# Block transposes on VectorE and another row order of the weights in a mixture-of-experts layer

## The reference, cut to what matters

```python
def clamped_swiglu(gu):
    gate, up = gu[..., :D_FF], gu[..., D_FF:]
    gate = jnp.minimum(gate, 7.0)
    up = jnp.clip(up, -7.0, 7.0)
    return (up + 1.0) * (gate * jax.nn.sigmoid(gate * 1.702))

# 32 experts, each token goes to its 4 best; D_MODEL = D_FF = 1024
def expert_block(args):
    xblk, e = args
    act = clamped_swiglu(xblk @ w_gate_up[e] + b_gate_up[e])   # 1024 -> 2048 -> 1024
    return act @ w_down[e] + b_down[e]
```

## Time and profile before

| | us |
|---|---|
| three runs, median (lowest to highest) | 1427.42 (1425.87 to 1429.18) |
| the profiled execution, its device time | 1427.33 |
| its span, first to last instruction | 1425.6 |
| experts, first to last matmul of L661 and L687 | 321.96 to 1386.4 |
| PE busy | 1286.2 (90%) |
| DVE / ACT / POOL busy | 496.2 / 324.7 / 299.4 |
| moved by DMA | 454.86 MB, mean 319 GB/s |

### The profile page before, as it was taken

One profiled execution on the slowest core, in us unless ns is written; L12 is line 12 of the kernel. 1 busy time (PEld: TensorE's weight loads), 2 busy tenths in 40 slices (PEclk: granted clock), 3 DMA queues, 4 the chain that ended last, 5 costly groups with the idle time before them and its releaser, 6 DMA issues.

```text
span 1425.6 us, 33985 instructions
## 1 busy us (share of the span) xinstructions
PE 1286.2 (90%) x12484; PEld 560.1 (39%) x12485; DVE 496.2 (35%) x1476; ACT 324.7 (23%) x649; POOL 299.4 (21%) x348
## 2 busy tenths in 40 slices
PE   6999999959998999999999999888999899988870
PEld 3764544543333434444444333333443333433320
DVE  2002222443334333333333344342334333343337
ACT  2023332221312222222222222221223222222211
POOL 0513332011212212222212112130212212111210
PEclk9999999969999999999999999999999999999995
DMA  9512110224999999999989999998999989999967
GB/s 379 208 59 74 60 74 1 104 83 173 415 386 415 394 413 395 368 365 366 366 366 365 392 418 416 417 416 352 366 367 417 413 362 414 393 417 416 417 248 294
DMA packets 90869, 454.86 MB, mean 319 GB/s; under 512 B 14049, under 2 KB 14489, under 8 KB 55774
## 3 DMA queue, kind: packets, MB, share of 16 engines
q1 hardware_dynamic: 77902, 430.86, 74.5%
q0 software_dynamic: 12512, 22.11, 4.3%
q10 hardware_dynamic: 432, 1.57, 0.3%
HBM read 444.23 MB, written 14.71 MB: 322 GB/s over the span
## 4 chain that ended last, share of the span: by engine, by line
PE 73%; DMA 21%; DVE 3%; issue 1%; ACT 1%; POOL 0%; SPq 0%; DVEq 0%; POOLq 0%
PE bank L661 35%; DMA arena<-in_w_gate_up 20%; PE bank L687 14%; PE bank L421 7%; PE bank L491 4%; PE bank L437 3%; PE bank L648 2%; PE bank L626 2%; PE bank L706 1%; PE bank L450 1%; DVE xs L1284 1%; PE bank L478 1%; PE bank L464 1%; PE bank L707 1%; PE bank L616 1%
## 5 line engine op out<-in xcount | busy, mean ns | idle before, releaser
L661 PE MATMUL bank<-arena,hT 128*32 128x512 f32 x5120 | 583.9, 606 | 30.2 <-DMA arena<-in_w_gate_up 27.9
L687 PE MATMUL bank<-arena,hT 128*32 128x256 f32 x5120 | 308.4, 386 | 33.1 <-ACT hT L859 33.1
L661 PEld LDWEIGHTS bank<-arena,hT 128*32 128x32 f32 x5120 | 157.3, 111 | 393.0 <-issue 341.1
L1241 DVE TENSOR_TENSOR arena<-bank,gain 128x512 f32<-128x512 f32 x128 | 88.4, 691 | 402.0 <-PE bank L661 402.0
L687 PEld LDWEIGHTS bank<-arena,hT 128*32 128x32 f32 x5120 | 159.6, 111 | 161.3 <-issue 77.3
L963 POOL DMA_DIRECT2D ahead<-in_consts x98 | 51.6, 530 | 641.1 <-DVE hT L1260 615.3
L876 ACT ACTIVATE arena<-arena 128x256 f32<-128x256 f32 x128 | 53.3, 417 | 560.1 <-DVE arena L1243 558.7
L1260 DVE TENSOR_TENSOR hT<-bank,gain 128x256 f32<-128x256 f32 x128 | 51.4, 422 | 212.2 <-PE bank L687 206.1
L980 POOL DMA_INDIRECT y_rows<-hT,arena x80 | 82.4, 1029 | 158.3 <-DVE hT L1260 150.7
L421 PE MATMUL bank<-hT,arena 128*128 128x512 f32 x224 | 103.6, 610 | 0.8 <-ACT hT L764 0.8
L966 POOL DMA_INDIRECT hT<-h_rows,arena x82 | 84.8, 1035 | 67.9 <-issue 34.0
(11 more groups left out here) (146 smaller groups left out, 857.9 us busy)
## 6 DMA issues: line engine op xcount, KB each, us to landing
arena<-in_w_gate_up SPq DMA_DIRECT2D x256, 1024.0 KB, 6.6
arena<-in_w_down SPq DMA_DIRECT2D x128, 1024.0 KB, 15.3
arena<-in_w_in SPq DMA_DIRECT2D x10, 1024.0 KB, 18.1
arena<-y_rows SPq DMA_DIRECT2D x8, 1024.0 KB, 12.3
arena<-in_w_out SPq DMA_DIRECT2D x4, 1024.0 KB, 22.0
arena<-bias_by_dist POOLq DMA_DIRECT2D x6, 512.0 KB, 4.0
xs<-in_x SPq DMA_DIRECT2D x4, 512.0 KB, 7.4
h_rows<-arena POOLq DMA_DIRECT2D x4, 512.0 KB, 2.9
```

The source lines that it names most:

```text
L661: mm = pe.matmul(bank[c][j * CH:(j + 1) * CH, :].rearrange("p (g n) -> p g n", g=2), xT[:, c, (k % 2) * P + (k // 2) * CH:(k % 2) * P + (k ...
L687: mm = pe.matmul(bank[c][j * CH:(j + 1) * CH, 0:Q], aT[:, c, (k % 2) * P + (k // 2) * CH:(k % 2) * P + (k // 2 + 1) * CH], w[:, j * Q:(j + ...
L1241: dve.tensor_tensor(gu[:, b, :], bank[c][:, :], bt[:, 0:2 * Q], ALU.add).then_inc(gu_read, 1)
```

## The change

PE no longer transposes or multiplies biases in the jobs, and ACT no longer copies. DVE turns each chunk with one instruction that transposes 32 x 32 blocks, SBUF to SBUF. A block transpose leaves quarter j on partitions 32 j to 32 j + 31. With its input read at a step of eight values (32 bytes), what stands on partition p for step k is weight row 8 p + k, so the weights are read in that order: partition p of gate unit k holds weight row 8 p + k (8 KB, from one partition to the next 64 KB apart in HBM), and of down unit u rows 8 p + 2 u and 8 p + 2 u + 1 (8 KB in one piece, 32 KB apart). The biases of one expert are fetched by a DMA of four rows of 3 KB, issued by ACT, and spread over the 32 partitions of each quarter by one DVE shuffle of 128 x 768. Chunks that are absent do no work on any engine: the semaphores count chunks, not four for each job, and two more rows of the job table carry the running counts. Each engine loads more of them into registers in a job: PE three instead of one, DVE six instead of two. The rows of the next job are turned on DVE between the last activation and `job_columns`.

```diff
@@ load_unit @@
-                    src = w_gate_up[bass.ds(e, 1), u * P:(u + 1) * P, :].rearrange("e p n -> p (e n)")
-                    dst = ring[:, u, :]
+                    src = w_gate_up[bass.ds(e, 1)].rearrange("e (p k) n -> (e k) p n", p=P)[u]
                 else:
-                    a = (u - KT) * 2 * P
-                    src = w_down[bass.ds(e, 1), a:a + 2 * P, :].rearrange("e (k p) n -> p (e k) n", p=P)
-                    dst = ring[:, u, :].rearrange("p (k n) -> p k n", k=2)
+                    src = w_down[bass.ds(e, 1)].rearrange("e (p u k) n -> (e u) p (k n)", p=P, k=2)[u - KT]
+                dst = ring[:, u, :]
@@ PE, run_job @@
-                pe.wait_ge(t_copied, job * NCH + 1)
-                pe.wait_ge(pick_done, job + 1)
-                pe.matmul(bank[4][:, 0:2 * Q], pick, bias_all[:, 0:2 * Q], start=True, stop=True).then_inc(bias_mm, 1)
-                pe.matmul(bank[5][:, 0:Q], pick, bias_all[:, 2 * Q:3 * Q], start=True, stop=True).then_inc(bias_mm, 1)
-                pe.wait_ge(x_copied, job * 2 + 2)
+                every = range(KT)
                 indices(job + 1)
+                pe.wait_ge(x_done, job + 1)
                 with pe.If(chunks > 2):
                     with pe.If(chunks > 3):
                         gate(3, every)
...
+                    gate(2, every)
+                gate(1, every)
+                gate(0, every)
                 with pe.If(chunks > 2):
                     with pe.If(chunks > 3):
                         down(3, every)
...
+                    down(2, every)
+                down(1, every)
                 down(0, every)
             njobs = pe.value_load(njobs_i[0:1, 0:1], min_val=E, max_val=JOBS_MAX - 2)
             with pe.Fori(0, njobs) as job:
-                run_job(job, pe.value_load(jobs_i[0:1, 2, bass.ds(job, 1)], min_val=1, max_val=NCH))
+                run_job(job, pe.value_load(jobs_i[0:1, 2, bass.ds(job, 1)], min_val=LEAST, max_val=NCH),
+                        pe.value_load(jobs_i[0:1, 3, bass.ds(job, 1)], min_val=2, max_val=COUNT_MAX),
+                        pe.value_load(jobs_i[0:1, 3, bass.ds(job + 1, 1)], min_val=4, max_val=COUNT_MAX))
@@ ACT @@
+            def load_bias(e):
+
+                act.dma_start(bias_row[0:P:CH, :], biases[bass.ds(e * 4, 4), :])\
+                    .then_inc(bias_in, 16)
...
+                act.wait_ge(bias_spread, job + 1)
+                load_bias(e)
@@ DVE @@
+            def flip_x(c, last):
+
+                ins = dve.transpose(xT[:, c, :], xg[:, c, :].rearrange("p (i k) -> p k i", k=KT))
...
+                def swiglu(c):
...
+                    dve.tensor_tensor(act_q[b], up, sg[:, b, :], ALU.mult).then_inc(actq_done, 1)
+                    dve.wait_ge(actq_done, low + (AHEAD - c))
+                    dve.transpose(aT[:, c, :], act_q[b].rearrange("p (i k) -> p k i", k=KT)).then_inc(act_done, 1)
...
+                dve.wait_ge(y_done, before_job + AHEAD)
+                dve.wait_ge(bias_in, job * 16 + 16)
+                dve.stream_shuffle(bt, bias_row[:, :], [0] * CH).then_inc(bias_spread, 1)
+                job_rows(job + 1, link_job)
+                dve.wait_ge(bias_spread, job + 1)
+                with dve.If(chunks > 2):
+                    with dve.If(chunks > 3):
+                        swiglu(3)
+                    swiglu(2)
+                swiglu(1)
+                swiglu(0)
+                dve.wait_ge(gathered, rows_in)
+                with dve.If(next_chunks > 2):
+                    with dve.If(next_chunks > 3):
+                        flip_x(3, False)
+                    flip_x(2, False)
+                flip_x(1, False)
+                flip_x(0, True)
                 job_columns(after, job + 2, link_job)
-                for c in range(NCH):
-                    dve.wait_ge(scattered[c], job * 16 + 16)
+                dve.wait_ge(scattered, before_job * 16)
...
-                for n, c in enumerate(ORDER):
-                    dve.wait_ge(dn_done, job * NCH + (n + 1))
+                with dve.If(chunks > 2):
+                    with dve.If(chunks > 3):
+                        add_bias(3)
+                    add_bias(2)
+                add_bias(1)
+                add_bias(0)
```

More of the change, by code:

```diff
@@ L65 @@
 FREED = JOB_UNITS - 2
-ORDER = tuple(range(NCH))[::-1]
+LEAST = 2
+AHEAD = NCH - 1
 JOBS_MAX = 49
+COUNT_MAX = 2 + NCH * JOBS_MAX
 FAR = 4096
@@ L672, in gate, with down @@
                             mm.then_inc(units_used, 1)
-                        if k == 5 and flip is not None:
-                            flip_act(flip)
-                def down(c, ks, absent=0):
-                    n = ORDER.index(c)
-                    if 0 in ks:
-                        pe.wait_ge(t_copied, job * NCH + (n + 2))
+                def down(c, ks):
+                    pe.wait_ge(act_done, low + (AHEAD - c))
                     for k in ks:
@@ L903, in link @@
                 pool.wait_ge(pstep, steps[0])
-            for c in range(NCH):
-                pool.dma_start(ahead[0:16, 1, c, :], consts[0:16, 4 * c:4 * c + 4])\
-                    .then_inc(scattered[c], 16)
+            for a in range(2):
+                pool.dma_start(ahead[0:16, a, :], consts[0:16, 4 * a:4 * a + 4]).then_inc(scattered, 16)
+            pool.memset(bias_row[:, :], 0.0).then_inc(bias_zero, 1)
             link(pool.memset(pb[:, :, 0:8], 0.0))
@@ L998, in _ @@
                 pool.sem_inc(waited_pool, 1)
-                gather(next_chunks)
-                for n, c in enumerate(ORDER):
-                    pool.wait_ge(y_done, job * NCH + (NCH + n + 2))
-                    pool.sem_inc(waited_pool, 1)
-                    if c == 0:
-                        scatter_chunk(c)
-                        continue
-                    with pool.If(chunks > c):
-                        scatter_chunk(c)
-                    with pool.If(chunks <= c):
-                        signal(c, scattered[c], 1)
@@ L1010, in _ @@
-            for c in range(NCH):
-                pool.wait_ge(gathered[c], njobs * 16 + 16)
+                with pool.If(next_chunks > 2):
+                    with pool.If(next_chunks > 3):
+                        gather(3, gathered)
+                    gather(2, gathered)
+                gather(1, gathered)
+                gather(0, gathered)
+                with pool.If(chunks > 2):
+                    with pool.If(chunks > 3):
+                        scatter(3)
+                    scatter(2)
@@ L1217, in _ @@
                 .then_inc(gate_in, 1)
+            def flip_x(c, last):
+                ins = dve.transpose(xT[:, c, :], xg[:, c, :].rearrange("p (i k) -> p k i", k=KT))
+                if last:
+                    ins.then_inc(x_done, 1)
+            dve.wait_ge(gathered_first, 16 * NCH)
+            for c in range(NCH):
+                flip_x(c, c == NCH - 1)
             job_columns(1, None, link)
-            job_picker(0)
             link(dve.tensor_copy(keep_s, idx_t[:, :, 1]))
```

261 lines of the change are left out of this document (103 added, 158 removed).

## The result

The changed kernel takes 1406.28 us (median of 4 runs, 1404.44 to 1407.78) where the kernel before, run beside it, takes 1426.91 us: ratio 0.9853, 95% interval 0.9835 to 0.9871. It is 20.6 us faster, less than half of the 45 us that the prediction gave it: about 25 us of the forecast gain are missing. The profiled execution took 1407.16 us with a span of 1405.4 us.

The account below looks back on a forecast made before the run. PE was taken to bound three-chunk jobs, weight transfers two-chunk jobs. Stage -39 us, last job -4.3 and start -1.5, together -45 against 1427.33, gave 1382 us; range 1357 to 1412.

Parts of the forecast that it names:

- The likeliest case: Whole kernel: the forecast itself holds, with a time of 1370 to 1400 us; chance 0.60.
- the case that did hold 1400 to 1424: Whole kernel: DVE or gathers as a partial bound, or a pitch that costs up to 3%; chance 0.13.
- the pitch: Rival, weight transfers: 64 KB steps could collide in HBM, 1481 us at 10%; slower by this or long DVE chain, chance 0.10.
- the idle at a job's start: PE at each job start: two more register loads leave the array idle about 0.65 us, 1.0 at most.
- just in time: Three-chunk job after a handover: SP issues at 9.3 us, DMA has down units for 10.5 us, data follows within 2 us.
- The stage: First free gate slot to last handover: 968 us for bytes plus 4 and 14 us, 986 us, or -39.
- The array's own work: PE in a three-chunk job without flips and bias matmuls: 31.4 to 31.9 us, taken as 31.5.
- The lead of 0.3 us: PE's sequencer at a job start: runs some 0.3 us ahead, set against 0.97 us for two more loads.
- DVE as the bound: Rival: PE waits for DVE once a transpose takes 1.55 us; 1424 us at 2.2 us, half of it 1403.
- No effect: Rival, whole kernel: saved PE time is lost to waits one for one, 1427 us; chance 0.03.
- The floor of DMA alone: Rival, whole kernel: loads hidden, clock up, down units gain, only bytes count, 1357 us; chance 0.14.
- its 4 and 14: Stage: 8 three-chunk jobs behind three-chunk jobs at 32.1 instead of 31.6, 4 us; 7 behind two-chunk jobs at 2 us, 14.

Follow-up runs that it names:

- the first experiment: Changed kernel with only the chunk count loaded at a job's start, two table loads moved between gate groups and the bias-add wait moved too: 1393.67 us.
- The filler: Changed kernel with 20 unused matmuls placed between and behind the three register loads at each job start on PE: 1406.68 us, ratio 0.9841.
- the experiment on the row order: Kernel before with only the new order of weight rows in its transfers, output not the reference's: 1418.11 us, ratio 0.9944.
- slots and late loads: Changed kernel with second slots for gate units 0 to 5, gate code in two arms, and two table loads moved off the job start: 1364.56 us.
- the two failed forms of spare slots: Changed kernel with six more ring slots and SP and PE loops unrolled by two: 1485.19 us; the same with table loads moved off the job start: 1536.41 us.

## Why the prediction was wrong, point by point

The direction held, and so did part of the mechanism: PE lost its flips and biases and three-chunk jobs became shorter, by 2.1 us. 1406 us is inside the range of 1357 to 1412, but by luck. The likeliest case, 1370 to 1400, missed, and the case that did hold 1400 to 1424 rested on DVE or the pitch, which had no part in it. Two steps failed. The first is the idle at a job's start: 0.6 us were taken and the array stands for 1.7 us, with a slow clock behind it in some jobs, where the prediction had the clock fall behind waits for weights alone. Gaps at a job's start far from 0.6 us were one of its own signs of being wrong. The second is the rest of DMA that comes from one slot for each unit: it was taken at 2 us, and "just in time" otherwise, and is 3.8 us in a pair of jobs. The profiled execution is 25.2 us over 1382. The terms, one by one:

**The stage.** Forecast 986 us from the first free slot to the last handover; the trace has it from 337.87 to 1351.17, 1013.3 us, 27 us more. It falls into two parts and a rest.

*Three-chunk jobs behind three-chunk jobs*, forecast 32.1 us, measured 33.84: 8 x 1.74 = 14 us. Three errors lie in it.
- The array's own work: from a gate start to the end of down 31.17 us and 0.55 for the index matmuls, so 31.7, where 31.5 was taken: 0.2 us.
- The idle at the start: on average 1.5 us ahead of the index matmuls and 0.2 behind them, 1.7 where 0.6 was taken: 1.1 us. The price of a load came from the earlier trace rows, which shows a lone load with one register operation; each further load brings its own address operation too and takes 0.7 to 0.8 us instead of 0.48. The lead of 0.3 us that was set against it didn't cover the loads when the old kernel got them, where the idle is 1.4 us. And with only one load at the start, in the first experiment, 0.6 us of idle remain, where the prediction had none; what they are was not looked into. That the loads make up the greater part of this idle, the two experiments show from both sides: -12.6 us when they move (with a wait that moves along), +14 us when the old kernel gets them.
- The clock after the idle: 1.7 us in two of the eight jobs (the periods of 35.24 and 34.94 us), 0.4 us a job. The filler shows that in this kernel an idle of about 1.5 us, with nothing to do with weights, can bring it about. The Trainium skill (TensorE: Matmul & The Clock Gate, What's actually happening) has the gated clock as the default that activity lifts, and the trace of this case agrees as far as it goes: 0.50 at the start of a slow group and 1.00 after that. The prediction cited it and did not ask where the change itself makes the array rest.

*Pairs of a three-chunk and a two-chunk job*, forecast 2 x 31.6 + 2 = 65.2 us, measured 66.5 on average over five pairs: 7 x 1.3 = 9 us, if the two that stand beside runs of three-chunk jobs lose as much. The mechanism was as told, a clock below 1 behind the handover, slots freed late, DMA resting. Its size was not: taken were 2 us of rest and "just in time" at a full clock; at the saturated rate of this kernel the pair wastes 66.5 - 62.7 = 3.8 us. The issue came 1.4 and 2.5 us late, near the 2 us. But the one pair that kept its clock, in the first experiment, took 64.7 us, 2.0 above the bytes' 62.7, where the prediction had some 63.2 for a full clock. So about half of the 3.8 us is the clock behind the wait and half is there without it: "just in time" was wrong by some 1.5 us. Only one pair ran at a full clock, but the other nine of the kernel after and of the first experiment line up with it: with the 136 matmuls at 16.1 to 16.3 us a pair takes 65.8 to 66.0, and at 17.2 to 17.4 us 66.7 to 67.7.

*The rest.* The two parts make 23 of the 27 us. Another 3.6 us lie ahead of the first handover: from 337.87 to 394.15 are 56.3 us, for 20 units that need 52.7 us at 31.6 us a job. What they consist of was not looked into.

**The floor.** 968 us at 416 GB/s; the saturated stretches now run at 418 to 420, 961 us. The row order, costed at nothing with a bound of -7, measured -8 us in the old kernel. It went to the faster side and hides in the sum above.

**Start and tail.** First gate matmuls at 319.82 where 320.9 was forecast and 321.96 stood before; the first SP issue comes 2.5 us earlier, forecast 1.5. From the last handover to the last scatter are 1367.89 - 1351.17 = 16.7 us instead of 22.5, so -5.8 us, forecast -4.3. These two are 1.0 and 1.5 us better than forecast and take back 2.5 of the 27 us: 27.3 - 2.5 = 24.8, and the miss is 25.2.

**DVE.** Right. The transposes take 0.59 to 0.67 us, inside 0.425 to 0.74, and the shuffle 1.03, below its bounds of 1.3 to 2.2. PE never waits for them, and doubled transposes don't change the time. By the rule of the Trainium skill on Memory Cachelines (Advanced Engine Details and Errata) a stepped access is penalised. The prediction drew from it that a transpose would lie at 0.74 us or above, and none does: at 0.62 us against the 0.425 of a 256-value row there is room for a penalty of a half but not for a doubling. What an unstepped transpose takes no run here shows. The cover is thin behind two-chunk jobs, as the twelve waits of the first experiment show, but there the weights set the pace.

**The rivals.** The pitch fell with the experiment on the row order. DVE as the bound fell with the doubled transposes. No effect, 1427 us, fell with the result. The floor of DMA alone, 1357 us, had the small distance of PE and DMA for it and the slow rows behind waits against it; the latter was right. With slots and late loads 1364.56 us are reached, 7 us of it by an earlier start of loading that the floor does not have. So most of the way to the floor is open, and two things stood on it that the prediction priced at 18 us (its 4 and 14) and that cost 42 - 7 = 35 (1406.3 - 1364.6, less the earlier start).

**What stays open.** The halving of the 3.8 us rests on one pair at a full clock. Why the slow gate groups behind an idle start come in some jobs of the changed kernel and not in others, and in none of the old kernel with two more loads, why 0.6 us of idle are left with one load, and why the two failed forms of spare slots differ by some 50 us, was not found.

## What to carry to other kernels

Price a sequencer's work at a loop's start by all of its rows, register operations and branches included, against how far that sequencer runs ahead there, and place loads behind work that is queued on the array: moving two of them gave 12.6 us here. When PE and DMA come within a few per cent of each other, the number of free slots decides more than either's speed, so look for the stretch in which DMA rests while PE is busy. A pause of the array that a change adds costs its own length and can cost, in the group behind it, some of the clock.

## What the runs showed of the hardware that was not expected

- An idle of 1.3 to 1.8 us at a job start is followed in 6 of 16 unbroken cases by a gate group that is 1.7 us slower, with no transfer waited for; with the idle filled, down to 0.2 us, it is 0 of 16. In the old kernel with two more loads an idle of 1.4 us ahead of the bias matmuls slowed none of 30 groups.
- A loop body on PE of sixteen blocks of one chunk instead of eight had 3.00 MB of instructions fetched instead of 0.23 MB and stood for some 10 us at each back edge; with nine blocks it was 0.23 MB again and 1.3 to 2.3 us.
- One and the same table load costs 0.48 us when it is alone, and 0.7 to 0.8 us for each that follows.
- Rows at a pitch of 64 KB, 8 KB of each, are moved at 419 to 420 GB/s, no slower than consecutive rows at 417; a short stretch with the 4 KB pieces of the old down units had 408.
